# S5 chunk inputs in two column halves with reversed moving columns, router logits on four column strips, and the first expert unit's rows picked from on-chip memory

## What is computed

```
def s5_mixer(hn, ...):
    u = hf.reshape(b, s, S5_GROUPS, S5_GROUP_SIZE)          # 64 groups of 16
    y = (_s5_one_direction(u, a_re[0], a_im[0], ...)
         + _flip(_s5_one_direction(_flip(u), a_re[1], a_im[1], ...)))
    ...
def moe_swiglu(h, w_router, w_gu, w_down):
    logits = (xt @ w_router).astype(F32)                    # 512 x 8
    top_logit, top_e = lax.top_k(logits, TOP_K)
    gates = jax.nn.softmax(top_logit, axis=-1)
    ...                                                     # rows sorted by expert, in blocks
    y_buf = lax.map(expert_block, (x_buf.reshape(...), blk_e))
    out = jnp.zeros((t, d)).at[tok_buf].add(y_buf * w_buf[:, None])
```

## Time and profile before

| what | value |
|---|---|
| runs, median (lowest to highest) | 2479.22 us (2478.05 to 2483.16), three runs |
| the profiled execution's own time | 2480.71 us |
| its span, first to last instruction | 2479.1 us |
| mean granted PE clock | 0.979 of full |
| PE, DVE, ACT, POOL busy | 95%, 65%, 50%, 8% |
| chain that ended last, by engine | PE 82%, DVE 10%, ACT 2%, issue 2%, POOL 2%, DMA 2% |

### The profile page before, as it was taken

One profiled execution on the slowest core, in us unless ns is written; L12 is line 12 of the kernel. 1 busy time (PEld: TensorE's weight loads), 2 busy tenths in 40 slices (PEclk: granted clock), 3 DMA queues, 4 the chain that ended last, 5 costly groups with the idle time before them and its releaser, 6 DMA issues.

```text
span 2479.1 us, 35658 instructions
## 1 busy us (share of the span) xinstructions
PE 2366.9 (95%) x14674; PEld 1821.0 (73%) x14674; DVE 1604.0 (65%) x1790; ACT 1234.5 (50%) x1306; POOL 201.0 (8%) x214
## 2 busy tenths in 40 slices
PE   7999999999999999679889999999999999999988
PEld 4555555788888887678667788777887788777866
DVE  7997678422223334693456688667876688667866
ACT  3645344322222232753245577556765577556754
POOL 4007634000000000000000000000000000000010
PEclk9999999999999999789889999999999999999998
DMA  7668311522332323433187899779997799878962
GB/s 194 202 203 239 97 59 35 187 95 92 102 101 94 102 102 103 174 131 134 62 288 270 287 383 357 281 270 329 376 326 272 273 371 372 280 272 303 381 232 88
DMA packets 259810, 527.98 MB, mean 213 GB/s; under 512 B 19526, under 2 KB 61098, under 8 KB 256986
## 3 DMA queue, kind: packets, MB, share of 16 engines
q1 hardware_dynamic: 230250, 481.30, 55.2%
q0 software_dynamic: 6208, 25.78, 3.4%
q10 hardware_dynamic: 23184, 18.55, 2.3%
HBM read 496.03 MB, written 45.81 MB: 219 GB/s over the span
## 4 chain that ended last, share of the span: by engine, by line
PE 82%; DVE 10%; ACT 2%; issue 2%; POOL 2%; DMA 2%; ACTq 0%; POOLq 0%; DVEq 0%
PE psum L1958 38%; PE psum L1446 17%; PE psum L1783 6%; PE psum L2000 4%; PE psum L2022 2%; PE psum L1321 2%; PE psum L1725 1%; PE psum L1518 1%; PE psum L2029 1%; DVE stages L866 1%; DVE stages L876 1%; DVE stages L871 1%; DVE stages L867 1%; POOL stages L1115 1%; PE psum L2126 1%
## 5 line engine op out<-in xcount | busy, mean ns | idle before, releaser
L1958 PE MATMUL psum<-stages_r 128*128 128x512 f32 x4032 | 958.0, 396 | 0.0
L3662 DVE TENSOR_TENSOR stages_r<-kept,stages_r 128x2048 fp32r<-128x2048 f32 x336 | 769.7, 2291 | 284.8 <-ACT stages_r L2621 284.3
L1958 PEld LDWEIGHTS psum<-stages_r 128*128 128x128 f32 x4032 | 752.0, 189 | 180.1 <-issue 21.4
L2621 ACT ACTIVATE stages_r<-kept 128x2048 fp32r<-128x2048 f32 x336 | 644.1, 1917 | 365.0 <-PE psum L1958 352.0
L1446 PE MATMUL psum<-stages_r 128*128 128x512 f32 x1920 | 437.5, 390 | 3.2 <-ACT stages_r L2170 2.7
L1446 PEld LDWEIGHTS psum<-stages_r 128*128 128x128 f32 x1920 | 360.1, 188 | 79.3 <-ACT stages_r L2170 3.1
L3318 DVE TENSOR_TENSOR stages_r<-kept,stages_r 128x2048 fp32r<-128x2048 f32 x54 | 123.8, 2293 | 341.9 <-ACT stages_r L2479 341.9
L2479 ACT ACTIVATE stages_r<-kept 128x2048 fp32r<-128x2048 f32 x54 | 103.6, 1918 | 329.4 <-PE psum L1446 219.0
L1783 PE MATMUL psum<-stages_r,stages_front_r 128*128 128x512 f32 x672 | 152.6, 389 | 0.8 <-issue 0.8
L1783 PEld LDWEIGHTS psum<-stages_r,stages_front_r 128*128 128x128 f32 x672 | 126.1, 188 | 27.3 <-issue 1.2
L1321 PE MATMUL psum<-stages,kept 128*128 128x512 f32 x256 | 115.5, 598 | 0.0
(11 more groups left out here) (481 smaller groups left out, 2412.6 us busy)
## 6 DMA issues: line engine op xcount, KB each, us to landing
kept<-in_moe_w_gu_dram SPq DMA_DIRECT2D x224, 1024.0 KB, 6.9
kept<-in_moe_w_down_dram SPq DMA_DIRECT2D x112, 1024.0 KB, 6.5
kept<-in_ffn_w_gu_dram SPq DMA_DIRECT2D x28, 1024.0 KB, 5.1
kept<-in_ev_w_in_dram SPq DMA_DIRECT2D x16, 1024.0 KB, 7.9
kept<-in_ffn_w_down_dram SPq DMA_DIRECT2D x14, 1024.0 KB, 5.0
s_output_maps<-s_output_maps_by_state SPq DMA_DIRECT2D x32, 256.0 KB, 4.8
kept<-s_input_maps SPq DMA_DIRECT2D x8, 1024.0 KB, 5.0
kept<-s_output_maps SPq DMA_DIRECT2D x8, 1024.0 KB, 5.9
```

The source lines that it names most:

```text
L1958: m = pe.matmul(out_, a, b, start=start and n == 0, stop=stop and n == len(pairs) - 1, skip_group_check=True)
L2621: act.activation(w_high[n % WSLOTS], unit_tile(n), ACT.Copy).then_inc(s_wh, 1)
L3662: dve.tensor_tensor(w_low[n % WSLOTS], unit_tile(n), w_high[n % WSLOTS], ALU.subtract).then_inc(s_ws, 1)
```

## The change

- **S5 chunk inputs.** Each product of a group is split in two: the matrix's columns for the forward direction stream `U`'s 64 columns in order into PSUM partitions 0 to 63, its columns for the backward direction stream them from last to first (an access pattern with step -1) into partitions 64 to 127. Nothing is streamed twice any more. The bank then has both halves in the same order, and ACT moves it with one activation on 128 partitions where it took two on 64.
- **Router.** The router tile has 32 columns per k (8 weights, the rest zeros set by POOL ahead of its DMA). The logits of the four token chunks go to four column strips of one bank, all behind the last `turn_chunk`, in 32 matmuls. One copy and one 128 x 128 transpose replace four of each.
- **First unit's rows.** As soon as the ranks are there, DVE works out which tokens belong to the busiest expert (`first_rank`), and writes a one-hot table `pick_rows` (512 tokens x 160 slots). PE multiplies `hn4` with it (32 float32 matmuls of 160 columns), which gives the first unit's rows already turned; ACT and DVE copy them out. The gather of unit 0 and its `turn_rows` are gone, and SP no longer waits for it.
- **The rest of the plan later.** What remains of the plan (`rows_of_slots`, `slot_choices`, `finish_plan`) stands behind steps 0, 1 and 2 of the first unit on DVE; the slot list's matmuls (`slot_tokens`) ahead of step 5 on PE, its copy on DVE in step 5. POOL waits for it with the gather of unit 1.
- Semaphores are merged or counted differently, and the one-hot tables live elsewhere.

```diff
@@ POOL: router
-            pool.dma_start(router, I["moe_router"][0].rearrange("(k p) e -> p k e", p=P)).then_inc(s_rtr, 16)
+            chain.link(pool.memset(router, 0.0))
+            chain.settle()
+            pool.dma_start(router[:, :, 0:NE], I["moe_router"][0].rearrange("(k p) e -> p k e", p=P)).then_inc(s_rtr, 16)
@@ POOL: first gather
             pool.wait_ge(s_mys, FILLED)
-            gather_rows(0)
@@ SP: expert tiles
-                    if first_unit and n == WSLOTS:
-                        sp.wait_ge(s_xg, gathers_done(0))
@@ PE: chunk_inputs
                     for gl in range(4):
+                        forward = U[:, 8 * q + 4 * i + gl, :]
+                        backward = bass.AP(sbuf, base + (8 * q + 4 * i + gl) * NC5 + NC5 - 1, [[words, P], [-1, NC5]])
                         for e in range(2):
                             x = 2 * gl + e
-                            times = 2 if x < 7 else 1
-                            m = pe.matmul(psum[:, b % 8, x * NC5:(x + times) * NC5].rearrange("p (a n) -> p a n", a=times),
-                                          w[:, 4 * i + gl, e, :],
-                                          U[:, 8 * q + 4 * i + gl, :].unsqueeze(1).broadcast_to([P, times, NC5]), start=True,
-                                          stop=True)
+                            for d, u in enumerate((forward, backward)):
+                                m = pe.matmul(psum[NS * d:NS * (d + 1), b % 8, x * NC5:(x + 1) * NC5],
+                                              w[:, 4 * i + gl, e, NS * d:NS * (d + 1)], u, start=True, stop=True)
@@ PE: router
             turn_chunk(4, 2)
+            turn_chunk(4, 3)
             pe.wait_ge(s_rtr, 16)
-            logits(0)
-            turn_chunk(4, 3)
-            for c in range(1, TC):
-                logits(c)
-            for c in range(TC):
-                pe.wait_ge(s_parTd, c + 2)
-                m = pe.transpose(psum[:, 5, NE * c:NE * (c + 1)], lg_rows[0:NE, c * P:(c + 1) * P], ident[0:NE, 0:NE])
+            pe.wait_ge(s_hA, 4 * (TURN[4] + 1))
+            pe.wait_ge(s_hD, 4 * (TURN[4] + 1))
+            for k in range(8):
+                for c in range(TC):
+                    m = pe.matmul(psum[strip(c), 4, 0:P], router[:, k, :], hnT[:, k, c * P:(c + 1) * P],
+                                  start=k == 0, stop=k == 7, skip_group_check=True)
             m.then_inc(s_lg, 1)
+            pe.wait_ge(s_parTd, 2)
+            pe.transpose(psum[:, 5, 0:P], lg_rows, ident).then_inc(s_lg, 1)
@@ PE: behind the ranks
+            pe.wait_ge(s_slot, 2)
+            for bank, k0, k1 in PICK_BANKS:
+                for k in range(k0, k1):
+                    for c in range(TC):
+                        m = pe.matmul(psum[:, bank, (k - k0) * CAP:(k - k0 + 1) * CAP], hn4[:, c, k * P:(k + 1) * P], pick_rows[:, c, :],
+                                      start=c == 0, stop=c == TC - 1, skip_group_check=True)
+                m.then_inc(s_xtp, 1)
...
+                    if i == 0 and s_ == 5:
+                        slot_tokens()
...
-            turn_rows(0)
@@ ACT: chunk_inputs
-                for d in range(2):
-                    first, step = (z_at[v] + g, QW) if d == 0 else (NS * words + z_at[v] + (NC5 - 1) * QW + g, -QW)
-                    m = act.activation(bass.AP(sbuf, first, [[words, NS], [1, 4], [ZW // 2, 2], [step, NC5]]),
-                                       bank[NS * d:NS * (d + 1)], ACT.Copy)
-                m.then_inc(s_vd, 1)
+                act.activation(bass.AP(sbuf, z_at[b // 4] + 4 * (b % 4), [[words, P], [1, 4], [ZW // 2, 2], [QW, NC5]]),
+                               psum[:, b % 8, :].rearrange("p (g e n) -> p g e n", g=4, e=2), ACT.Copy).then_inc(s_vd, 1)
@@ ACT: ahead of the first unit
+            act.wait_ge(s_lg, 1)
+            act.activation(slot_junk[:, 4:5], eps, ACT.Silu)
             split(0, 0)
+            for n, (bank, k0, k1) in enumerate(PICK_BANKS):
+                act.wait_ge(s_xtp, n + 1)
+                rows = psum[:, bank, 0:(k1 - k0) * CAP].rearrange("p (q t) -> p q t", t=CAP)
+                act.activation(x_rest[0][:, k0:k1, :], rows[:, :, P:CAP], ACT.Copy)
+                act.activation(xb[0][:, k0:k1, 0:P], rows[:, :, 0:P], ACT.Copy).then_inc(s_xtA, 1)
             split(0, 1)
-            act.wait_ge(s_plan, 1)
-            act.activation(slot_junk[:, 4:5], eps, ACT.Silu)
-            rows_high(0)
             split(0, 2)
@@ DVE: behind plan_e
+            for n, before in ((1, 1.0), (2, P + 1.0)):
+                chain.link(dve.tensor_scalar(first_rank[:, n, :], first_rank[:, 0, :], -before, None, ALU.add))
+            chain.settle()
+            for c in range(TC):
+                chain.link(dve.tensor_scalar(pick_rows[:, c, 0:P], rowi, first_rank[:, 1, c:c + 1], None, ALU.is_equal))
+                chain.link(dve.tensor_scalar(pick_rows[:, c, P:CAP], rowi[:, 0:REST], first_rank[:, 2, c:c + 1], None, ALU.is_equal))
+            chain.settle()
+            dve.tensor_copy(topf[:, :, 0], first_rank[:, 0, :]).then_inc(s_slot, 1)
@@ DVE: in the first unit, at the end of a step
+                        if s_ == 0:
+                            rows_of_slots()
+                        elif s_ < 3:
+                            slot_choices(s_ - 1)
+                        if s_ == 2:
+                            finish_plan()
```

221 lines of the change are left out of this document (121 added, 100 removed).

## The result

| | before | after |
|---|---|---|
| runs, median (lowest to highest) | 2481.19 us (2478.05 to 2483.18), four runs | 2462.85 us (2462.12 to 2464.70), four runs |
| the profiled execution: time, span | 2480.71, 2479.1 us | 2462.12, 2459.9 us |
| mean granted PE clock | 0.979 | 0.982 |
| PE, DVE, ACT busy | 95%, 65%, 50% | 96%, 65%, 49% |

The ratio after to before is 0.9929, 95% interval 0.9917 to 0.9940: 17.6 us less by it (14.9 to 20.6), 18.3 by the medians. Forecast were 2467.5 and a range of 2461 to 2474: the sign and the range hold. (One later execution of the kernel after took 10,814 us, over four times its neighbours; it is in no number here and unexplained.)

A forecast was written before the change was run, and what follows sets the result against it. PE was taken to bound nearly everything except at the S5 inputs and around the router. Gains 1.9 + 11.8 less 1.8 and 0.2 made 11.7: from 2480.7 to 2469.0, less 1.5 to the median, 2467.5 us; range 2461 to 2474.

The forecast's parts named there:

- both column halves side by side: Rival at the S5 chunk inputs: the two halves overlap in load and stream, gain 3.4 more, 2464.1 us; chance 0.16.
- S5 inputs: Chunk inputs on PE: load-bound passes of 0.057 us, 1.83 us a bank, so DVE's scan starts sooner; gain 1.9 us.
- Logits: Router: 64 passes on four column strips, 3.64 us at half clock; DVE reads 4.0 us sooner, 5.6 at full clock.
- Ranks, `plan_e`, tables: DVE behind the logits: ranks unchanged at 5.24 us, `plan_e` 2.02 plus 0.2 later, pick tables ready at 1232.0.
- Picks: First unit's rows on PE: 64 passes of 160 columns in 12.7 us, full clock after 7.5 us.
- DVE's arithmetic in step 0: First unit: 5.7 us of plan arithmetic moved there just fits ahead of the split of tile 7; 0.2 us counted.
- DVE's arithmetic makes PE wait: Rival in the first unit: PE stands 3 to 5 us in steps 1 and 2, 2471.5 us; chance 0.07.
- The slot list: Inside the PE-bound first unit: 16 passes with full loads and 20 columns, 1.8 us, all exposed.
- Given back: Losses in the first unit: 1.8 us for slot-list matmuls on PE and 0.2 us for DVE's plan arithmetic.
- Picks at half clock throughout: Rival at the first unit's rows: 5 us lost there and 2 for a cold unit start, 2474 us; chance 0.05.
- unit no earlier: Rival: an unseen tile or buffer still holds the first unit, leaving little but the S5 gain, 2477 us; chance 0.02.
- load not overlapping: Rival at the S5 inputs: loads do not overlap the other half's streams, total gain 3.3, 2475.9 us; chance 0.05.

The follow-up runs named there:

- the added chain: The changed kernel with twenty more small DVE operations, one after another, behind the plan's arithmetic in step 0 of the first unit; 2471.18 us.

## Why the prediction was right, and where it was not

- **The number.** 2462.85 lies in the range, 1.9 us above its lower end, and outside the forecast's own span of 2464 to 2471.5. What came is the rival *both column halves side by side*, with the picks at the short end of the forecast's 2 us either way; both terms erred to the same side. The range held because it took the rival in.
- **What bounds the kernel, and where.** Right: the gain came in the two stretches that the chain of waits had outside PE, and nothing between them moved (90.34 us from GLU to the third chunk in both).
- **S5 inputs: the step that failed.** "The loads are half of what they were and there are twice as many, so I take the load-bound value: 32 x 0.057." Measured 0.029 a pass with alternating halves, 0.058 when both products go to one half. The price of a pass on one half was right; that it adds to the other half's was the mistake, and the term was 5.3 to 6.0 at the scan, not 1.9. (Under *What would show it* the 128 passes should be 256; the 128 are matmuls.) The rival *both column halves side by side* had this, with its gain of 5.3, at a chance of 0.16. That chance was too low. The row for it was the earlier trace rows, 64 passes over four strips at 0.030 each; I noted that loads one after the other would give the same number, and then let the load-bound reading win without a row that spoke for it. The rule of the Trainium skill that was weighed there ("TensorEngine Tiling (Array Packing)", Theoretical Speedup, up to 2x for sides of 64 or less) is what the runs show: 0.058 / 0.029 = 2.0.
- **Kept to the end of the stage.** Right in the profiled execution, by luck: scan to GLU 107.34 and 107.25. In six of eight profiles with this code 1.6 of the gain went in a clock that fell behind a wait of PE, a cost that the prediction did not list.
- **Logits.** Forecast 4.0 at half clock and 5.6 at full; measured 4.1 to 4.2 at half, 5.6 to 6.9 at full.
- **Ranks, `plan_e`, tables.** Ranks forecast 5.24 behind the read of the logits, measured 5.34; `plan_e` 2.2 and 2.16; tables ready 18.3 after the third chunk and picks at 17.97.
- **Picks: mis-sized.** Forecast 12.7, measured 10.6 (10.5 to 11.5 in kernels that share the code and the wait ahead of it). The prices at either clock hold: 9.00 us at full clock, 0.141 a pass. What was off is when full clock returns, taken as 7.5 us from the earlier trace rows. The window 1228 to 1230, 2.1 us into the picks, shows 0.69 and the next 1.00:

```profile
1228.00:1230.00 2.00, 2.00 (x12) 2.00 (x11) 0.00 (x0) 0.00 (x0) 0.00 (x0) 0.69 1.05 402
```

Twelve passes at 0.277 and 52 at 0.14 give the 10.6, so it was about 3.3; by the same reckoning the 10.5 to 11.5 are 3.0 to 5.1 (an estimate). None comes to 7.5. The end was earlier by 2.1, as was the unit. The stage's gain was 14.5 and not 11.8; this term is most of the difference, the rest is 0.2 each of the logits, the picks' start and ACT's last copies.
- **DVE's arithmetic in step 0.** Right, closely: a margin forecast at 0.5, measured at 0.65 by the added chain. The rival *DVE's arithmetic makes PE wait* was one small chain away.
- **The slot list** on PE cost 1.78 where 1.8 was forecast:

```profile
1345.62 1.86 PE L1957 MATMUL psum<-stages 128*128 128x20 f32 x16
1347.40 1.95 PE L2005 MATMUL psum<-kept,stages 128*32 128x128 f32 x64
```

- **Given back.** Forecast 2.0 in all; from rest up to the end 1.0 was lost. The slot list's 1.8 is there in the row, so 0.8 was won somewhere in the units. Other profiles of the same code give 0.9 to 1.6, and where it comes from stays open.
- **Picks at half clock throughout, unit no earlier, load not overlapping:** none of them occurred.

The sum with the measured terms: 5.36 + 14.48 + 0.36 - 1.00 = 19.20 of span. With the picks as forecast and S5 as measured it would have been 2464.1, the side-by-side rival's number, 1.3 us off the median. By the gain it is further off, 15.1 against 18.3.

## What to carry to other kernels

Where an operand has 64 columns or fewer, alternate between the column halves matmul by matmul: here, with 64 columns loaded and 64 streamed in float32, that halved the price, and grouping eight matmuls a half gave most of it back. When a row fits two mechanisms equally well, it is no evidence for either, and each should get a chance of the same order until a row separates them. After a change that leaves PE bound, look at the granted clock behind each remaining wait of a few microseconds: filler matmuls that end when the real ones start were worth 0.3% here, more than the S5 part of the change.

## What the runs showed that I had not expected

- Loads and streams of float32 passes on two column halves run side by side in full: 0.029 us a pass of 64 columns against 0.058 on one half (windows of 2 us count 76 and 38), and 0.047 (46 to 48) when the half changes every 16 passes.
- A moving operand read with step -1 streams as fast as one read in order.
- When full clock returns behind an idle stretch is not fixed: without fillers the logits ran at full clock in three of eight profiles of the same code and at half clock in five, and the picks took 10.5 to 11.9 us. One execution's wait for full clock is a poor price for another stretch.
- Two executions can do nearly the same and get another clock. Ahead of the GLU PE was busy 0.99 and then 1.21 of 2 us (windows from 1102 on) in the kernel after, and the clock stayed at 1.00; in the kernel with the block arithmetic ahead of the tables it was 0.99 and 1.22, and the clock fell to 0.93 in the second window and to 0.50 behind it.
